# Turning normalised rows on TensorE: transposes of scaled rows, or fp32 products of unscaled rows with a diagonal

## What is computed

```
y = xf * lax.rsqrt(jnp.mean(xf * xf, axis=-1, keepdims=True) + EPS)
return y * g          # first block
h = modulate(rmsnorm(x, g), shift, scale)   # second block: h * (1 + scale) + shift
```

## Time and profile before

| | |
|---|---|
| median of 3 executions | 1164.64 us (1161.25 to 1164.98) |
| the profiled execution's own time | 1164.23 us |
| span of its trace | 1162.4 us |
| TensorE matmul busy | 1085.8 us (93%), weight load 888.6 us (76%) |
| VectorE busy | 743.5 us (64%) |
| ScalarE busy | 495.9 us (43%) |
| mean granted clock of TensorE | 0.981 of full speed |
| HBM | 204.88 MB moved, 176 GB/s on average |

### The profile page before, as it was taken

One profiled execution on the slowest core, in us unless ns is written; L12 is line 12 of the kernel. 1 busy time (PEld: TensorE's weight loads), 2 busy tenths in 40 slices (PEclk: granted clock), 3 DMA queues, 4 the chain that ended last, 5 costly groups with the idle time before them and its releaser, 6 DMA issues.

```text
span 1162.4 us, 19633 instructions
## 1 busy us (share of the span) xinstructions
PE 1085.8 (93%) x8492; PEld 888.6 (76%) x8492; DVE 743.5 (64%) x1153; ACT 495.9 (43%) x770; POOL 33.7 (3%) x31
## 2 busy tenths in 40 slices
PE   5999979897999997999899999999899899999997
PEld 5884579895768776697657889999657677998995
DVE  6761967747569948666467677667437656554544
ACT  2422222133454467355254555354333555554442
POOL 0000005300000010000000000000000000000000
PEclk9999989999999999999899999999999999999999
DMA  9763200522257450363434567766743545474620
GB/s 388 275 247 130 88 2 3 220 76 75 94 196 269 165 217 2 140 232 136 181 130 164 227 251 294 289 276 226 281 145 145 217 145 178 184 264 171 217 74 36
DMA packets 15078, 204.88 MB, mean 176 GB/s; under 512 B 1800, under 2 KB 1800, under 8 KB 2832
## 3 DMA queue, kind: packets, MB, share of 16 engines
q1 hardware_dynamic: 14544, 202.55, 46.2%
q10 hardware_dynamic: 448, 1.08, 0.2%
HBM read 202.57 MB, written 1.05 MB: 175 GB/s over the span
## 4 chain that ended last, share of the span: by engine, by line
PE 76%; DVE 15%; ACT 3%; issue 2%; DMA 2%; SPq 0%; DVEq 0%; ACTq 0%
PE bank L432 15%; PE bank L434 15%; PE bank L433 15%; PE bank L391 5%; PE bank L700 5%; PE bank L490 5%; DVE slot_parts L1749 2%; PE bank L547 2%; DMA ring<-in_stream 1%; PE bank L503 1%; PE bank L517 1%; PE bank L610 1%; DVE arena L1877 1%; PE bank L682 1%; DVE small L1723 1%
## 5 line engine op out<-in xcount | busy, mean ns | idle before, releaser
L432 PE MATMUL bank<-page_parts 128*128 128x512 f32 (+1 forms) x1104 | 378.3, 343 | 4.9 <-DVE page_parts L1782 2.5
L1749 DVE TENSOR_TENSOR slot_parts<-ring,page_parts 128x2048 fp32r<-128x2048 f32 x104 | 236.9, 2288 | 120.6 <-ACT page_parts L1194 120.3
L1194 ACT ACTIVATE page_parts<-ring 128x2048 fp32r<-128x2048 f32 x104 | 197.7, 1910 | 139.8 <-PE bank L434 88.0
L432 PEld LDWEIGHTS bank<-page_parts 128*128 128x128 f32 x1104 | 210.4, 191 | 29.7 <-issue 4.3
L433 PE MATMUL bank<-slot_parts,page_parts 128*128 128x512 f32 x576 | 225.6, 392 | 0.0
L434 PE MATMUL bank<-page_parts 128*128 128x512 f32 x576 | 225.5, 391 | 0.0
L1251 ACT ACTIVATE arena<-bank 128x512 f32<-128x512 f32 (+1 forms) x142 | 78.7, 572 | 211.4 <-PE bank L490 66.6
L433 PE MATMUL bank<-page_parts 128*128 128x256 f32 x528 | 149.4, 283 | 0.0
L434 PE MATMUL bank<-page_parts,slot_parts 128*128 128x256 f32 x528 | 149.4, 283 | 0.0
L434 PEld LDWEIGHTS bank<-page_parts 128*128 128x128 f32 x576 | 108.9, 189 | 23.2
L433 PEld LDWEIGHTS bank<-slot_parts,page_parts 128*128 128x128 f32 x576 | 109.2, 190 | 21.6
(11 more groups left out here) (285 smaller groups left out, 1230.6 us busy)
## 6 DMA issues: line engine op xcount, KB each, us to landing
ring<-in_stream SPq DMA_DIRECT2D x95, 2048.0 KB, 8.3
arena<-in_x SPq DMA_DIRECT2D x2, 512.0 KB, 4.4
gn<-in_gn ACTq DMA_DIRECT2D x2, 512.0 KB, 13.0
out<-arena SPq DMA_DIRECT2D x2, 512.0 KB, 2.6
cc<-in_consts SPq DMA_DIRECT2D x1, 898.0 KB, 6.6
pc<-in_params SPq DMA_DIRECT2D x1, 287.5 KB, 6.9
gn<-in_head_sel ACTq DMA_DIRECT2D x1, 32.0 KB
pos_i<-in_positions ACTq DMA_DIRECT2D x1, 1.0 KB, 4.0
```

The source lines that it names most:

```text
L432: mm(out, a[0], b[0], start=start, stop=False)
L1194: act(unit_parts(n)[0], unit_values(n)[1], ACT.Copy).then_inc(ac.step("w_hi"), 1)
L1749: tt(unit_parts(n)[1], lo, hi, ALU.subtract).then_inc(dv.step("w_lo"), 1)
```

## The change

The row scaling is left out. In its place VectorE multiplies the 128x128 identity, which lies in the constants, by the same inverse roots: two diagonals `ROOTS`, in the first 256 columns of page 13. TensorE then computes for each tile the fp32 product of the unscaled `X` tile (the stationary operand) with the diagonal of its token half (the moving one), which is the tile turned and scaled. The products stand in the place of the transposes, in the same order, with the same waits and the same banks. In the first normalisation VectorE's wait for the constants comes ahead of `norm` now, since it reads the identity there.

```
+        ROOTS = arena[:, 13, 0:2 * P].rearrange("p (b n) -> p b n", b=TB)
...
+            def turned_rows(name):
+
+                for i in range(KT // 2):
+                    b = claim((name, i))
+                    for jj in range(2):
+                        for tb in range(TB):
+                            j = 2 * i + jj
+                            ins = mm(b[:, jj * T + tb * P:jj * T + (tb + 1) * P], X[:, tb, j * P:(j + 1) * P], ROOTS[:, tb, :],
+                                     start=True, stop=True)
+                    ins.then_inc(filled((name, i)), 1)
...
             pe.wait_ge(sem("xn"), 2)
-            transposes("hT_a", XN)
+            turned_rows("hT_a")
...
                 for tb in range(TB):
-                    ts(XN[:, tb, :], X[:, tb, :], ss[:, tb:tb + 1], None, ALU.mult).then_inc(dv.step("xn"), 1)
+                    ts(ROOTS[:, tb, :], ident, ss[:, tb:tb + 1], None, ALU.mult).then_inc(dv.step("xn"), 1)
...
             dve.wait_ge(*dv.last)
-            dve.wait_ge(sem("x_loaded0"), 16)
+            dve.wait_ge(sem("loads"), 48)
             norm()
-            dve.wait_ge(sem("loads"), 48)
```

More of the change, by code:

```diff
@@ L886, in _ @@
             pe.wait_ge(sem("xn"), 4)
-            transposes("hT_b", XN)
+            turned_rows("hT_b")
             ada_turned()
@@ L930, in mlp @@
                 pe.wait_ge(sem("xn"), 8 + 4 * l)
-                transposes(f"hT_m{l}", XN)
+                turned_rows(f"hT_m{l}")
                 ada_turned()
@@ L979, in _ @@
             pe.wait_ge(sem("xn"), 6)
-            transposes("hT_c", XN)
+            turned_rows("hT_c")
             ada_turned()
@@ L1069, in _ @@
             pe.wait_ge(sem("xn"), 10)
-            transposes("hT_d", XN)
+            turned_rows("hT_d")
             ada_turned()
```

## The result

The changed kernel takes 1168.12 us, the median of 20 executions (1162.58 to 1174.08), against 1162.69 us for 20 of the kernel before (1157.31 to 1166.08). The ratio is 1.0045 with a 95% interval of 1.0032 to 1.0058: slower by 5.2 us (3.7 to 6.7). The forecast was +4.5 us.

A forecast was written before the change was run, and what follows sets the result against it. TensorE's queue was taken to bound the kernel. The places summed as 0.7 + 0.4 + 1.6 + 0.7 + 0.4 + 0.7 = +4.5 us on 1164.2, so 1168.7 us, range 1166 to 1172, chance 0.75.

The forecast's parts named there:

- Which places wait: Of six places, TensorE waited for VectorE's scaling only at the start and ahead of the two MLPs; saving 0.94 us a place.
- `hT_m0` and `hT_m1`: Ahead of the two MLPs: TensorE starts 0.94 us earlier, works 1.77 longer, had 0.16 slack; +0.7 us each.
- The price of a product: At each place: a product is two records, a transpose one; 32 records take 3.74 us against 1.97, 1.77 us more.
- fourth rival: All six places: a product costs four passes, 0.45 us, about +25 us, 1190 us in all; chance 0.02.
- `hT_c`: Place where filler hides the scaling: TensorE's queue becomes the later one before the projection, 1.77 - 0.16 = +1.6 us.
- `hT_b` and `hT_d`: Places where filler hides the scaling: ScalarE's copies start later, TensorE's extra work mostly hidden; +0.4 us each.
- `hT_a`: First normalisation, at the lower clock: earlier start, doubled records, clock rising 4.5 us after first work; +0.7 us (-0.5 to +2.3).
- early clock rise: First rival, at the start: products raise the clock sooner than transposes; +3.3 or +2.8 us in all; chance 0.2.
- cheap product: Second rival, all places: a product costs hardly more than a transpose; -2.8 us at one pass, 1161.4 us; chance 0.03.
- third rival: Clock drop near 839 us, varying between executions: 1.7 us either way with or without the change; no chance of its own.

## Why the prediction was right

- **Which places wait.** Right in all six: the shorter scaling let TensorE start 0.94 us sooner at `hT_m0` and `hT_m1` and 0.99 at the start, and gave nothing at the other three.
- **The price of a product.** Two records, 32 a place, 3.84 us for the 3.74 of the sum. The pace is 0.115 us a record ((3.84 - 0.28)/31) instead of 0.112; the factor of two holds. The fourfold price of the fourth rival is refuted, by the 3.84 us and by the doubled products.
- **`hT_c`** +1.65 for +1.6, **`hT_m0` and `hT_m1`** +0.7 each as forecast, **`hT_b` and `hT_d`** +0.5 each for +0.4. At `hT_d` I gave the pace to ScalarE alone. In the trace after, TensorE does not wait for it any more: line 491 begins at 851.65 and its 32 records run without the two waits of 0.26 us for ScalarE that were there before. Its own queue sets the end of the place about as late as ScalarE's copies do, so the sum does not notice. That the number fits there is partly luck.
- **`hT_a`** is the term that was too small: +0.7 in the sum, +1.1 in the profiled pair. The step that failed was to take one execution's clock rise (the first record of full length 4.5 us after the first work) for both kernels. In the profile after it came 5.4 us after it, and 0.9 us more at the lower level, at about half speed, are the missing 0.4. Over twelve traces the delay was 3.3 to 6.1 us, with either kind of work, so what failed was the certainty and not the way the term was added up. The 1.7 us over five traces and the 2.3 (1.0 to 3.5) by timing have the scatter of the clock in them; how much more than the sum's 0.7 the place costs on average stays open.
- **The rivals.** The early clock rise (0.2) did not come: the second panel began at 30.77 us, 64 transposes raised the clock by themselves, and the soonest rise with products was 3.3 us after the first. The sentence of the Trainium skill, page "TensorE: Matmul & The Clock Gate", section Part 4: PE-mode transpose, that transpose mode does not engage the full clock, does not agree with the trace of the 64 fp32 transposes, which went from 421 ns to 272 ns each. The cheap product (0.03) was excluded by the pace. The third rival's drop of the clock at 839 us came again in the profile after (8.72 us for the filler) and explains nothing of the difference.
- **The size.** It was +5.2 us (3.7 to 6.7) by timing and +5.15 place by place, for +4.5 forecast. Of the 0.65 us between the sums, 0.4 are `hT_a`, and `hT_b`, `hT_d` and `hT_c` make the rest. The prediction has no term for the clock later in the program, which may be worth about 1 us; that the timing and the places agree to 0.1 us is chance within that interval.

## What to carry to other kernels

An operation moved to the engine that bounds the kernel pays for every record there, while what it saves on another engine counts only where the bound engine had waited for it: here 0.94 us at three of six places against 1.9 us more of TensorE's queue at all six, of which the two places paced by ScalarE and VectorE hid most. Count records, not calls: an fp32 product with 128 columns is two of about 0.113 us at full clock where an fp32 transpose is one. And where TensorE waited for whole rows to be scaled, giving it the first half early took 0.46 us off a place (4.11 us against 4.57 at `hT_m0`) with no new work for it.

## What the runs showed of the hardware

In a row of nothing but fp32 transposes TensorE's clock went from its lower to its full level 5.4 us after the first one. In the twelve traces here the first record of full length came 3.3 to 6.1 us after TensorE's first work, and two kernels that begin with the same 64 products had it 3.3 and 5.6 us after: a sum that rests on one such rise is open by more than 1 us. The granted clock of a window reads 1.00 from 12 to 16 us in the profile after and from 15.0 to 17.2 us in the run with 64 transposes, where 128-column records of 421 ns and 0.21 us apart show the lower level: early in these traces the durations tell it, not that column. A VectorE scaling of 128x512 took 0.42 us where one of 128x1024 took 0.71, so cutting an instruction in two costs about 0.13 us.

A product in fp32r on the rounded residual was not tried; no run here shows what it would cost in this place.
